# Norm weights on x, feature block by feature block, in place of norm weights on the matrices

## The chip, the cores and the metric

The kernel runs on one core of a Trainium2 chip, as one launch. The metric is the device time of an execution in microseconds (us). A core has TensorE (PE in the profile: matmuls, and transposes against an identity matrix), ScalarE (ACT), VectorE (DVE), GpSimd (POOL) and a queue that issues DMA transfers (SP). Each engine works through its own list in order and waits for the others on semaphores.

## What is computed

Four transformer layers over 256 tokens of width 1024, all in fp32. Layers 0 and 1 are a differential attention and a neighbourhood attention, layers 2 and 3 a stick-breaking and a forgetting attention. Each layer has three RMS norms, one ahead of the attention, one ahead of the feed-forward part and one ahead of a gated side input:

```python
def rmsnorm(x, g, eps=NORM_EPS):
    xf = x.astype(jnp.float32)
    y = xf * lax.rsqrt(jnp.mean(xf * xf, axis=-1, keepdims=True) + eps)
    return (y * g.astype(jnp.float32)).astype(x.dtype)

h = h + attention(rmsnorm(h, norm_mix[i]))
h = h + swiglu(rmsnorm(h, norm_ffn[i]), w_gate[i], w_up[i], w_down[i])
gate = jax.nn.sigmoid(rmsnorm(h, norm_ple[i]) @ ple_w_gate[i])
h = h + gate * (p[i] @ ple_w_proj[i])
```

The weight g of a norm has one number for each of the 1024 features, and the matrix that follows is contracted over those features. So g may scale the normed input or the rows of the matrix: the product is the same. The fourth layer's first norm feeds matrices with two different weights (its own for the queries, a shared one for keys and values).

## The kernel before

**Halves.** Every fp32 operand of a large matmul is split into two fp32r tensors, a high half (a rounded copy) and a low half (the rest). A product is then three matmuls: high by high, high by low, low by high (`three`, L1618 to L1620; `across_unit` has the same three at L1729 to L1731). ACT makes the high half, DVE the low half from the source and the high half.

**Units.** The matrices stream in as units of 128 partitions x 1024 columns. SP loads a unit into one of six slots of `raw`, ACT makes `whi` from it (L830, `split`), DVE makes `wlo` (L1138 or L1140), and PE spends twelve matmuls on it and frees its slot. ACT works four units ahead of PE and DVE three, by the program order of each engine (`split_ahead`). `unit_parts` says in which column ranges a unit is split and which column of `gain` (the norm weights, one per partition) scales each. Most units hold two feature blocks of 512 columns, so with a norm weight they need two instructions of 512 columns on each engine. A gate unit has one block of 1024 columns. A unit without a norm weight takes one instruction of 1024 columns.

**x.** The input of a norm's matmuls, h transposed, lies in `xhi` and `xlo` as eight blocks of 128 features x 256 tokens. `turn_x` makes it in four quarters (q0 to q3: half the features and one of the two token tiles each). PE transposes four 128x128 blocks of h into one of two PSUM buffers (`turn`, L1779), ACT copies the buffer to `xhi` in one instruction of 512 columns (L861), DVE subtracts for `xlo` in one more (`lo_half`, L1160). The factor 1/rms (`rstd`) is applied later, to the product. The first norm of layer 0 has no transposes: x is loaded already transposed (`split_x`, L986 and L1439). `NORMS` are written (layer, n) with n = 0 for the attention, 1 for the feed-forward part and 2 for the gate.

**Order around a norm.** Program order on each engine decides everything here:

- n = 0 of layers 1 to 3, at the end of the layer before. ACT: sigmoid of gate bank 0 and 1 (L1117), x q0, sigmoid 2, x q1, sigmoid 3, a unit, x q2 and q3. DVE (`gated_side`): product and sum into h for banks 0 and 1 (L1184, L1186), x q0, product and sum 2, x q1, product and sum 3, a unit, x q2 and q3. PE: transposes of q0 and of q1 between the last gate matmuls, twelve matmuls on tile 0 (`first_pair`), transposes of q2 and q3, twelve matmuls on tile 1. The transpose of q3 waits for the sum of bank 3.
- n = 1, after the output projection: the same, with one sum into h (`add_to_h`, L1175) for each bank in place of product and sum, and no sigmoid.
- n = 2: transposes of q0 and q1 after the first half of the side projection, of q2 and q3 after its second half, then the gate units. The transpose of q3 also waits until DVE has read q1 out of the same PSUM buffer.

Until now PE waited for a whole quarter of x before its first block:

```python
def first_pair(L, n, s, behind):
    wait_out(pe, EV[("x", L, n, 0)])
    for t in range(T):
        if t:
            wait_out(pe, EV[("x", L, n, t)])
```

## Time and profile before

| | |
|---|---|
| median of 3 runs | 1314.66 us (1313.96 to 1315.85) |
| the profiled execution | 1316.3 us, its span 1314.5 us |
| PE busy | 1300.8 us, 99% of the span |
| DVE busy | 958.0 us, 73% |
| ACT busy | 847.8 us, 64% |
| HBM read | 238.33 MB, 182 GB/s over the span |
| granted clock of TensorE, mean | 0.999 of full speed |

The span runs from the first instruction to the last, the time of an execution also holds what lies around it. Busy time counts an instruction from start to end, and instructions of one engine overlap at their ends: a matmul of 512 columns is shown as 0.39 us long, but the next one starts 0.23 us after it. So the distance between starts says how fast an engine goes, and the sum of idle times says less than the page's percentages seem to.

### The profile page before, as it was taken

What the parts mean: (1) busy time and instruction counts of PE and PEld (TensorE: products, weight loads), DVE (VectorE), ACT (ScalarE), POOL (GpSimd) and SP (SyncE); (2) the same over time, 40 slices, a digit from 0 to 9 for tenths busy, and PEclk for the clock granted to TensorE, in tenths of its full rate; (3) what the DMA queues carried; (4) which work ended last, traced back from release to release, by engine and by line L of the source; (5) the groups of instructions that cost most, each with busy time, mean ns of one, the idle gap of its engine ahead of it and who ended that gap; (6) DMA issues with size and microseconds to landing.
All of it is one profiled execution on the core that took longest, in us unless ns stands there. A gap on an engine that the chain in (4) does not pass through costs nothing.

```text
span 1314.5 us, 20037 instructions
## 1 busy us (share of the span) xinstructions
PE 1300.8 (99%) x6642; PEld 1084.5 (83%) x6642; DVE 958.0 (73%) x1661; ACT 847.8 (64%) x1459; POOL 130.7 (10%) x179
## 2 busy tenths in 40 slices
PE   8999999999999999999999999999999999999998
PEld 7988888888887788888888888888887778888887
DVE  6887687666898766666699976666677887666664
ACT  7666666656777666665676666666578766666654
POOL 6031234410000000000010000000002210000000
PEclk9999999999999999999999999999999999999999
DMA  9444788876496566667647656666655535676671
GB/s 336 145 156 137 221 243 245 239 226 200 167 222 174 162 198 207 207 207 211 210 149 196 181 174 195 210 210 206 212 161 185 178 127 168 199 209 210 209 226 48
DMA packets 205056, 255.28 MB, mean 194 GB/s; under 512 B 72962, under 2 KB 163249, under 8 KB 204992
## 3 DMA queue, kind: packets, MB, share of 16 engines
q1 hardware_dynamic: 201984, 245.42, 60.8%
q0 software_dynamic: 2832, 8.49, 2.8%
q8 instruction: 37, 0.61, 0.2%
q10 hardware_dynamic: 176, 0.54, 0.1%
q14 instruction: 27, 0.22, 0.1%
HBM read 238.33 MB, written 1.13 MB: 182 GB/s over the span
## 4 chain that ended last, share of the span: by engine, by line
PE 92%; DVE 5%; ACT 1%; DMA 1%; issue 1%; SPq 1%; POOL 0%; DVEq 0%; ACTq 0%
PE acc L1618 14%; PE acc L1620 14%; PE acc L1619 14%; PE sc L1620 12%; PE sc L1619 12%; PE sc L1618 12%; PE turn L1779 3%; PE acc L1729 2%; PE acc L1730 2%; PE acc L1731 2%; PE turn L1881 1%; DVE wlo L1140 1%; DMA raw<-in_da_w_qkv 1%; PE sc L1832 1%; DVE z L1299 1%
## 5 line engine op out<-in xcount | busy, mean ns | idle before, releaser
L830 ACT ACTIVATE whi<-raw,aT_gain 128x512 fp32r<-128x512 f32 (+2 forms) x612 | 403.6, 719 | 79.1 <-PE sc L1620 53.4
L1140 DVE SCALAR_TENSOR_TENSOR wlo<-raw,aT_gain,whi 128x512 fp32r<-128x512 f32 (+2 forms) x612 | 431.0, 759 | 28.7 <-ACT whi L830 24.6
L1618 PE MATMUL sc<-whi,xhi 128*128 128x512 f32 x640 | 249.3, 390 | 0.0
L1620 PE MATMUL sc<-whi,xlo 128*128 128x512 f32 x640 | 249.0, 389 | 0.0
L1619 PE MATMUL sc<-wlo,xhi 128*128 128x512 f32 x640 | 249.0, 389 | 0.0
L1618 PE MATMUL acc<-whi,xhi 128*128 128x512 f32 x432 | 173.3, 401 | 1.8 <-DVE wlo L1140 1.4
L1620 PE MATMUL acc<-whi,xlo 128*128 128x512 f32 x432 | 168.5, 390 | 0.0
L1619 PE MATMUL acc<-wlo,xhi 128*128 128x512 f32 x432 | 168.5, 390 | 0.0
L830 ACT ACTIVATE whi<-raw 128x1024 fp32r<-128x1024 f32 x120 | 125.8, 1055 | 63.5 <-PE acc L1620 56.9
L1138 DVE TENSOR_TENSOR wlo<-raw,whi 128x1024 fp32r<-128x1024 f32 x120 | 145.5, 1244 | 0.0
L1619 PEld LDWEIGHTS sc<-wlo,xhi 128*128 128x128 f32 x640 | 120.1, 188 | 25.0
L1618 PEld LDWEIGHTS sc<-whi,xhi 128*128 128x128 f32 x640 | 120.1, 188 | 24.9
L1620 PEld LDWEIGHTS sc<-whi,xlo 128*128 128x128 f32 x640 | 120.1, 188 | 24.7
L1415 DVE SCALAR_TENSOR_TENSOR aT_gain<-sc,rstd,aT_gain 128x256 f32<-128x256 f32 x80 | 38.7, 484 | 114.7 <-ACT aT_gain L979 114.7
L979 ACT ACTIVATE aT_gain<-sc,rstd 128x256 f32<-128x256 f32 x80 | 38.0, 475 | 127.0 <-PE sc L1620 127.0
L1618 PE MATMUL acc<-whi,split_qg 128*128 128x512 f32 x288 | 112.4, 390 | 0.0
L1620 PE MATMUL acc<-whi,split_qg 128*128 128x512 f32 x288 | 112.1, 389 | 0.0
L1619 PE MATMUL acc<-wlo,split_qg 128*128 128x512 f32 x288 | 112.1, 389 | 0.0
L1618 PEld LDWEIGHTS acc<-whi,xhi 128*128 128x128 f32 x432 | 81.3, 188 | 19.0 <-DVE wlo L1140 1.9
L1620 PEld LDWEIGHTS acc<-whi,xlo 128*128 128x128 f32 x432 | 81.1, 188 | 17.4
L673 POOL TENSOR_SCALAR rstd<-ss 128x2 f32<-128x2 f32 x12 | 2.7, 222 | 917.3 <-ACT spare L853 917.3
L1619 PEld LDWEIGHTS acc<-wlo,xhi 128*128 128x128 f32 x432 | 81.4, 189 | 15.0
(213 smaller groups left out, 2069.6 us busy)
## 6 DMA issues: line engine op xcount, KB each, us to landing
raw<-in_ffn_w_gu SPq DMA_DIRECT2D x176, 256.0 KB
raw<-in_qk SPq DMA_DIRECT2D x62, 512.0 KB
raw<-in_ffn_w_gate SPq DMA_DIRECT2D x88, 256.0 KB
raw<-in_ffn_w_up SPq DMA_DIRECT2D x88, 256.0 KB
...
```

The costliest lines, as they stand in the source:

```text
L830: ins = act.activation(whi[:, u % RING, c0:c1], raw[:, u % RING, c0:c1], ACT.Copy, scale=scale)
L979: act.activation(aT[:, 0, t * 256:t * 256 + 256], bank[:, 0:256], ACT.Sigmoid, scale=rs(L, 1, t))\
L1138: ins = dve.tensor_tensor(lo, w, hi.bitcast(F32), ALU.subtract)
L1140: ins = dve.scalar_tensor_tensor(out=lo, in0=w, scalar=gain[:, g:g + 1], in1=hi.bitcast(F32), op0=ALU.mult, op1=ALU.subtract)
L1415: dve.scalar_tensor_tensor(out=sg, in0=banks[t][:, 256:512], scalar=rs(L, 1, t), in1=sg, op0=ALU.mult, op1=ALU.mult).then_inc(gmid, 1)
L1618: pe.matmul(dst, xh, wh, start=first, stop=False)
L1619: pe.matmul(dst, xh, wl, start=False, stop=False)
L1620: return pe.matmul(dst, xl, wh, start=False, stop=last)
L1729: pe.matmul(dst, wh, xh, start=first and k == 0 and c == 0, stop=False)
L1730: pe.matmul(dst, wl, xh, start=False, stop=False)
L1731: ins = pe.matmul(dst, wh, xl, start=False, stop=last and k == 1 and c == 1)
L1779: ins = pe.transpose(tb[e % 2][0:cols, n * rows:(n + 1) * rows], src, ident[0:rows, 0:rows])
```

## The change

All norm weights but those of the fourth layer's first norm move from the matrices to x. `unit_parts` returns a weight only for the units of that attention and for layer 0's output projection, whose weight belongs to another norm; every other unit becomes one part of 1024 columns without a weight. ACT and DVE now make each quarter of x in four instructions of 128 columns with the weight of their block (`x_gain`), in the fourth layer's first norm without one. ACT still signals once for a quarter, after its fourth block; DVE signals after each block, on the new semaphore `x_lo` for the first three and on `turn_out` for the last. PE waits per block (`wait_x`), in `first_pair` and in the gate units. In layer 0's first norm `split_x` goes by blocks of 256 columns.

```diff
...
@@ -287,26 +288,23 @@
 def unit_parts(L, s):
-    if s < U_WO:
+    if s < U_WO and L == L_FX:
         b = s % GROUP_UNITS
-        kv_gain = GAIN_SHARED if L == L_FX else GAIN_MIX[L]
         if b >= QK_UNITS:
-            at = kv_gain + V_UNITS * 2 * (s // GROUP_UNITS % 2) + 2 * (b - QK_UNITS)
+            at = GAIN_SHARED + V_UNITS * 2 * (s // GROUP_UNITS % 2) + 2 * (b - QK_UNITS)
             return [(512 * k, 512 * k + 512, at + k) for k in range(2)]
-        if L == L_FX:
-            return [(512 * k + 256 * x, 512 * k + 256 * x + 256, g + 2 * b + k)
-                    for k in range(2) for x, g in enumerate((GAIN_MIX[L], GAIN_SHARED))]
-        return [(512 * k, 512 * k + 512, GAIN_MIX[L] + 2 * b + k) for k in range(2)]
-    if s < U_GU0:
-        return [(0, 1024, GAIN_SUB if L == L_DA else None)]
-    if s < U_DOWN_LAST:
-        b = s - U_GU0 if s < U_FFN else (s - U_FFN) % 6
-        if b < 4:
-            return [(0, 512, GAIN_FFN[L] + 2 * b), (512, 1024, GAIN_FFN[L] + 2 * b + 1)]
-        return [(0, 1024, None)]
-    if s < U_GATE:
-        return [(0, 1024, None)]
-    return [(0, 1024, GAIN_PLE[L] + s - U_GATE)]
+        return [(512 * k + 256 * x, 512 * k + 256 * x + 256, g + 2 * b + k)
+                for k in range(2) for x, g in enumerate((GAIN_MIX[L], GAIN_SHARED))]
+    if L == L_DA and U_WO <= s < U_GU0:
+        return [(0, 1024, GAIN_SUB)]
+    return [(0, 1024, None)]
+
+
+def x_gain(L, n, kb):
+
+    if (L, n) == (L_FX, 0):
+        return None
+    return (GAIN_MIX, GAIN_FFN, GAIN_PLE)[n][L] + kb
 def build(nc, a, out):
...
@@ -463,6 +462,13 @@
         def p_halves(tile, L, t, h):
             return tile.bitcast(U16).rearrange("p (x c h) -> p x c h", c=S, h=2)[:, :, 0:keys(L, t), h]
+
+        def wait_x(eng, L, n, q, k):
+
+            if k == 3:
+                wait_out(eng, EV[("x", L, n, q)])
+            else:
+                eng.wait_ge(x_lo, 3 * (X_TURN[("x", L, n, q)] - 1) + k + 1)
         def scores_wait(eng, L, j, t):
...
@@ -858,8 +863,11 @@
                     hf, t = halves(q)
                     e = EV[("x", L, n, q)]
                     act.wait_ge(turned, e + 1)
-                    act.activation(xhi[:, 4 * hf:4 * hf + 4, t * P:(t + 1) * P],
-                                   tb[e % 2][:, :].rearrange("p (k c) -> p k c", k=4), ACT.Copy).then_inc(turn_hi, 1)
+                    for k in range(4):
+                        g = x_gain(L, n, 4 * hf + k)
+                        ins = act.activation(xhi[:, 4 * hf + k, t * P:(t + 1) * P], tb[e % 2][:, k * P:(k + 1) * P],
+                                             ACT.Copy, scale=1.0 if g is None else gain[:, g:g + 1])
+                    ins.then_inc(turn_hi, 1)
             def attention(L, name, j):
                 t = int(name[-1]) if name[-1] in "01" else 0
@@ -983,7 +991,10 @@
                 k0, k1 = X_PARTS[n]
                 act.wait_ge(x_t_in[n], 16)
-                act.activation(xhi[:, k0:k1, :], x_block(k0, k1), ACT.Copy).then_inc(x_t_hi, 1)
+                for kb in range(k0, k1):
+                    g = x_gain(0, 0, kb)
+                    ins = act.activation(xhi[:, kb, :], x_block(kb, kb + 1)[:, 0, :], ACT.Copy, scale=gain[:, g:g + 1])
+                ins.then_inc(x_t_hi, 1)
             for u in range(2):
                 split_x(u)
...
@@ -1163,9 +1172,16 @@
                 for q in quarters:
                     hf, t = halves(q)
                     e = EV[("x", L, n, q)]
-                    at = (slice(None), slice(4 * hf, 4 * hf + 4), slice(t * P, (t + 1) * P))
-                    lo_half(("x", L, n, q), xlo[at], xhi[at],
-                            tb[e % 2][:, :].rearrange("p (k c) -> p k c", k=4), e)
+                    dve.wait_ge(turn_hi, SPLIT[("x", L, n, q)])
+                    for k in range(4):
+                        g, at = x_gain(L, n, 4 * hf + k), (slice(None), 4 * hf + k, slice(t * P, (t + 1) * P))
+                        src = tb[e % 2][:, k * P:(k + 1) * P]
+                        if g is None:
+                            ins = dve.tensor_tensor(xlo[at], src, xhi[at].bitcast(F32), ALU.subtract)
+                        else:
+                            ins = dve.scalar_tensor_tensor(out=xlo[at], in0=src, scalar=gain[:, g:g + 1],
+                                                           in1=xhi[at].bitcast(F32), op0=ALU.mult, op1=ALU.subtract)
+                        ins.then_inc(x_lo if k < 3 else turn_out[e % 2], 1)
             def add_to_h(L, g, last, quarters):
                 for q in quarters:
@@ -1436,8 +1452,12 @@
                 k0, k1 = X_PARTS[n]
                 dve.wait_ge(x_t_hi, n + 1)
-                dve.tensor_tensor(xlo[:, k0:k1, :], x_block(k0, k1), xhi[:, k0:k1, :].bitcast(F32), ALU.subtract)\
-                    .then_inc(x_t_lo, 1)
+                for kb in range(k0, k1):
+                    g = x_gain(0, 0, kb)
+                    ins = dve.scalar_tensor_tensor(out=xlo[:, kb, :], in0=x_block(kb, kb + 1)[:, 0, :],
+                                                   scalar=gain[:, g:g + 1], in1=xhi[:, kb, :].bitcast(F32),
+                                                   op0=ALU.mult, op1=ALU.subtract)
+                ins.then_inc(x_t_lo, 1)
             for u in range(2):
                 split_x(u)
@@ -1664,10 +1684,7 @@
             def first_pair(L, n, s, behind):
-                wait_out(pe, EV[("x", L, n, 0)])
                 for t in range(T):
-                    if t:
-                        wait_out(pe, EV[("x", L, n, t)])
                     if GROUPS * L and n == 0:
                         pe.wait_ge(bank_out[t], GROUPS * L)
                     for b in range(2):
@@ -1675,6 +1692,7 @@
                         if t == 0:
                             ready(u)
                         for k in range(2):
+                            wait_x(pe, L, n, t, 2 * b + k)
                             ins = three(acc[t][:, :], xhi[:, 2 * b + k, t * P:(t + 1) * P],
                                         xlo[:, 2 * b + k, t * P:(t + 1) * P], whi[:, u % RING, 512 * k:512 * k + 512],
                                         wlo[:, u % RING, 512 * k:512 * k + 512], b == 0 and k == 0, False)
@@ -2000,9 +2018,8 @@
                     proj_unit(L, U_PROJ + b, b)
                     turn_x(L, 2, halves_at(b), lambda q: pe.wait_ge(bank_out[q], outs(q, L, G_DOWN + 1)))
                 for kb in range(KB - 2):
-                    if kb in (0, 4):
-                        for q in range(2):
-                            wait_out(pe, EV[("x", L, 2, q + (2 if kb else 0))])
+                    for t in range(T):
+                        wait_x(pe, L, 2, 2 * (kb // 4) + t, kb % 4)
                     wide_unit(L, U_GATE + kb, kb, xhi, xlo, kb == 0, False, G_GATE)
                 wide_last(L, U_GATE + KB - 2, KB - 2, xhi, xlo, G_GATE, behind_gate)
```

The order of the steps stays what it was; what stands at a place changes. DVE at the end of layer 0, from the first product of `gated_side` to the splits behind (`turn0`, `turn1` are the two PSUM buffers of the transposes, `aT_gain` holds the sigmoids and, in its last columns, the weights). Before:

```order
L1184 TENSOR_TENSOR aT_gain<-aT_gain,z 128x512
L1186 TENSOR_TENSOR h<-h,aT_gain 128x512
L1184 TENSOR_TENSOR aT_gain<-aT_gain,z 128x512
L1186 TENSOR_TENSOR h<-h,aT_gain 128x512
L1160 TENSOR_TENSOR xlo<-turn1,xhi 128x4x128
L1184 TENSOR_TENSOR aT_gain<-aT_gain,z 128x512
L1186 TENSOR_TENSOR h<-h,aT_gain 128x512
L1160 TENSOR_TENSOR xlo<-turn0,xhi 128x4x128
L1184 TENSOR_TENSOR aT_gain<-aT_gain,z 128x512
L1186 TENSOR_TENSOR h<-h,aT_gain 128x512
L1140 SCALAR_TENSOR_TENSOR wlo<-raw,aT_gain,whi 128x512 x2
L1160 TENSOR_TENSOR xlo<-turn1,xhi 128x4x128
```

Now:

```order
L1200 TENSOR_TENSOR aT_gain<-aT_gain,z 128x512
L1202 TENSOR_TENSOR h<-h,aT_gain 128x512
L1200 TENSOR_TENSOR aT_gain<-aT_gain,z 128x512
L1202 TENSOR_TENSOR h<-h,aT_gain 128x512
L1182 SCALAR_TENSOR_TENSOR xlo<-turn1,aT_gain,xhi 128x128 x4
L1200 TENSOR_TENSOR aT_gain<-aT_gain,z 128x512
L1202 TENSOR_TENSOR h<-h,aT_gain 128x512
L1182 SCALAR_TENSOR_TENSOR xlo<-turn0,aT_gain,xhi 128x128 x4
L1200 TENSOR_TENSOR aT_gain<-aT_gain,z 128x512
L1202 TENSOR_TENSOR h<-h,aT_gain 128x512
L1149 TENSOR_TENSOR wlo<-raw,whi 128x1024
L1182 SCALAR_TENSOR_TENSOR xlo<-turn1,aT_gain,xhi 128x128 x4
```

The products and sums stand where they stood; each `xlo` instruction of 4x128 columns has become four of 128, and each pair of 512-column splits one of 1024.

ACT at the same place, from the first sigmoid (`aT_gain<-acc0,rstd`). Before:

```order
L1117 ACTIVATE aT_gain<-acc0,rstd 128x512
L1117 ACTIVATE aT_gain<-acc1,rstd 128x512
L861 ACTIVATE xhi<-turn1 128x4x128
L1117 ACTIVATE aT_gain<-acc2,rstd 128x512
L861 ACTIVATE xhi<-turn0 128x4x128
L1117 ACTIVATE aT_gain<-acc3,rstd 128x512
L830 ACTIVATE whi<-raw,aT_gain 128x512 x2
```

Now:

```order
L1128 ACTIVATE aT_gain<-acc0,rstd 128x512
L1128 ACTIVATE aT_gain<-acc1,rstd 128x512
L868 ACTIVATE xhi<-turn1,aT_gain 128x128 x4
L1128 ACTIVATE aT_gain<-acc2,rstd 128x512
L868 ACTIVATE xhi<-turn0,aT_gain 128x128 x4
L1128 ACTIVATE aT_gain<-acc3,rstd 128x512
L836 ACTIVATE whi<-raw 128x1024
```

Each `xhi` copy has become four instructions with a weight, the first two of them still ahead of the sigmoids of banks 2 and 3.

PE in `first_pair` of layer 1's first norm, from the last transpose of q1 to the second block of tile 0, with the semaphores each waits for. Before:

```order
L1779 MATMUL turn0<-ident,h 128x128 x3
L1618 MATMUL acc0<-whi,xhi 128x512 [waits lo_done,bank_out0,turn_out1]
L1619 MATMUL acc0<-wlo,xhi 128x512
L1620 MATMUL acc0<-whi,xlo 128x512
L1618 MATMUL acc0<-whi,xhi 128x512
L1619 MATMUL acc0<-wlo,xhi 128x512
L1620 MATMUL acc0<-whi,xlo 128x512
L1618 MATMUL acc0<-whi,xhi 128x512 [waits lo_done]
```

Now:

```order
L1797 MATMUL turn0<-ident,h 128x128 x3
L1638 MATMUL acc0<-whi,xhi 128x512 [waits x_lo,lo_done,bank_out0]
L1639 MATMUL acc0<-wlo,xhi 128x512
L1640 MATMUL acc0<-whi,xlo 128x512
L1638 MATMUL acc0<-whi,xhi 128x512 [waits x_lo]
L1639 MATMUL acc0<-wlo,xhi 128x512
L1640 MATMUL acc0<-whi,xlo 128x512
L1638 MATMUL acc0<-whi,xhi 128x512 [waits x_lo,lo_done]
```

PE's list has the same matmuls; the wait for the whole quarter (`turn_out1`) has become a wait for `x_lo` at each block.

## Rows read from the trace of the kernel before

**Rows 1.** The page: span, and busy time, share and instructions of PE

```profile
span 1314.5 us, 20037 instructions
...
PE 1300.8 (99%) x6642; PEld 1084.5 (83%) x6642; DVE 958.0 (73%) x1661; ACT 847.8 (64%) x1459; POOL 130.7 (10%) x179
```

**Rows 2.** Who PE waited for: total us, times, longest

```profile
PE sc L1832 <- DVE split_qg L1349: 3.7, 2, 2.0
...
PE acc L1618 <- DVE wlo L1140: 1.4, 1, 1.4
```

**Rows 3.** Groups by line and shape: count | busy us, mean ns | idle before, releasers

```profile
L1140 DVE SCALAR_TENSOR_TENSOR wlo<-raw,aT_gain,whi 128x512 fp32r<-128x512 f32 x508 | 354.3, 754 | 20.9 <-ACT whi L830 16.8
L830 ACT ACTIVATE whi<-raw,aT_gain 128x512 fp32r<-128x512 f32 x508 | 331.7, 713 | 67.1 <-PE sc L1620 53.4 <-PE acc L1620 11.4 <-PE acc L1731 0.9
...
L830 ACT ACTIVATE whi<-raw 128x1024 fp32r<-128x1024 f32 x120 | 125.8, 1055 | 63.5 <-PE acc L1620 56.9 <-PE sc L1620 6.6
...
L1415 DVE SCALAR_TENSOR_TENSOR aT_gain<-sc,rstd,aT_gain 128x256 f32<-128x256 f32 x80 | 38.7, 484 | 114.7 <-ACT aT_gain L979 114.7
...
L1160 DVE TENSOR_TENSOR olo<-turn,ohi 128x256 fp32r<-128x256 f32 x16 | 6.1, 420 | 3.3 <-ACT ohi L1061 3.3
...
L1061 ACT ACTIVATE ohi<-turn 128x256 fp32r<-128x256 f32 x16 | 5.3, 382 | 12.3 <-PE turn L1779 12.3
...
L968 ACT ACTIVATE aT_gain<-turn 128x128 f32<-128x128 f32 x16 | 4.3, 273 | 15.7 <-PE turn L1861 15.7
...
L916 ACT ACTIVATE fin_gain<-turn,aT_gain 128x256 f32<-128x256 f32 x8 | 3.8, 472 | 9.9 <-PE turn L1779 9.9
```

**Rows 4.** ACT in order of time, end of layer 0: start us, us

```profile
333.43 0.60 ACT L861 ACTIVATE xhi<-turn 128x512 fp32r<-128x512 f32 x1 [1.11 <-PE turn L1779]
333.92 0.68 ACT L1117 ACTIVATE aT_gain<-acc,rstd 128x512 f32<-128x512 f32 x1
```

**Rows 5.** DVE in order of time, the same place

```profile
334.06 0.69 DVE L1160 TENSOR_TENSOR xlo<-turn,xhi 128x512 fp32r<-128x512 f32 x1 [0.26 <-ACT xhi L861]
334.67 0.68 DVE L1184 TENSOR_TENSOR aT_gain<-aT_gain,z 128x512 f32<-128x512 f32 x1
...
337.31 0.69 DVE L1186 TENSOR_TENSOR h<-h,aT_gain 128x512 f32<-128x512 f32 x1
```

**Rows 6.** PE in order of time, the same place

```profile
332.79 0.60 PE L1779 MATMUL turn<-ident,h 128*128 128x128 f32 x4
...
334.96 0.48 PE L1618 MATMUL acc<-whi,xhi 128*128 128x512 f32 x1
...
337.81 1.04 PE L1779 MATMUL turn<-ident,h 128*128 128x128 f32 x8
```

**Rows 7.** DVE and PE in order of time, second norm of layer 0

```profile
125.19 0.68 DVE L1175 TENSOR_TENSOR h<-acc,h 128x512 f32<-128x512 f32 x1
...
126.51 1.03 PE L1779 MATMUL turn<-ident,h 128*128 128x128 f32 x8
```

**Rows 8.** DVE and PE in order of time, third norm of layer 0

```profile
309.19 1.29 DVE L1160 TENSOR_TENSOR xlo<-turn,xhi 128x512 fp32r<-128x512 f32 x2 [1.96 <-ACT xhi L861]
...
311.50 1.03 PE L1779 MATMUL turn<-ident,h 128*128 128x128 f32 x8
```

**Rows 9.** ACT and PE in order of time, the first 30 us

```profile
11.68 1.34 ACT L830 ACTIVATE whi<-raw,aT_gain 128x512 fp32r<-128x512 f32 x2 [0.68 <-DMA raw<-in_qk]
...
27.20 0.38 PE L1832 MATMUL sc<-qkT 64*128 64x256 f32 x2 [0.26 <-DVE split_qg L1160]
```

**Rows 10.** DVE in order of time, attention of layer 1

```profile
385.95 1.41 DVE L1140 SCALAR_TENSOR_TENSOR wlo<-raw,aT_gain,whi 128x512 fp32r<-128x512 f32 x2
...
393.68 1.67 DVE L1349 SCALAR_TENSOR_TENSOR split_qg<-qkv,lam_in,qkT 128x256 fp32r<-128x256 f32 x4
...
413.05 1.22 DVE L1138 TENSOR_TENSOR wlo<-raw,whi 128x1024 fp32r<-128x1024 f32 x1
```

**Rows 11.** One stretch: length, busy us of each engine, granted clock, DMA share, GB/s

```profile
396.00:401.00 5.00, 5.00 (x40) 4.78 (x37) 5.00 (x21) 4.55 (x9) 0.00 (x0) 0.66 0.91 260
```

11 lines of the change are left out of this document (5 added, 6 removed).

## The prediction

> **What bounds the kernel now.** I read the page first. PE is busy for 1300.8 of 1314.5 us and DVE and ACT for 958.0 and 847.8 us [rows 1]; no matmul is added or removed, so the change can only shorten or lengthen what PE waits for. Then I read the list of PE's waits, which is short [rows 2]: 3.7 us in two places for the low half of q and k in layer 1's attention (2.0 and 1.7 us), and 1.4 us once for a low half of a matrix. The groups by shape [rows 3] give the price of each kind of instruction, and the engines in order of time [rows 4 to 10] show what stands in front of each wait and how much room there is where PE does not wait yet. The last view is the granted clock by stretch: it is 1.0 everywhere but behind the first of the two long waits, where five microseconds have a mean of 0.66 [rows 11]. That is (1 - 0.66) x 5 / 0.5 = 3.4 us at the lower of the two levels (1.2 in place of 2.4 GHz), which costs 1.7 us. It does not follow the second wait, of 1.7 us.
>
> **What the change takes away.** The 508 weighted splits of 512 columns [rows 3] are 254 units; all but the eight units of the fourth layer's v change. In each ACT's two instructions of 713 ns (a pair lasts 1.34 us [rows 9]) become one of 1055 ns [rows 3], and DVE's pair of 1.41 us becomes one of 1.22 us [rows 10]: 0.29 and 0.19 us less. Over 246 units that is 71 us of ACT and 47 us of DVE, and almost all of it is worth nothing, because both engines stand idle behind PE (ACT's 67.1 us of idle time ahead of these splits end with a release by PE in all but 2 us [rows 3]). It counts only in the few places where PE waits behind a split:
>
> - The start. Unit 2 lands, ACT splits it from 11.68 us on [rows 9], DVE follows, and PE waits 1.4 us [rows 2]. The chain becomes 0.29 + 0.19 = 0.48 us shorter. The next wait, 0.26 us at 27.20 [rows 9], stands behind more splits of both engines and goes. Together I take -0.7 us; all of it is lost if DMA, which carries the first units, is late, and it can't be above 1.7 us, which is both waits.
> - Layer 1's attention. Ahead of the first long wait DVE is busy without a gap for 11 us, and three pairs of weighted splits like the one at 385.95 stand in that row, ahead of the four `split_qg` at 393.68 [rows 10]: 3 x 0.19 = 0.57 us. Ahead of the second wait only one of three units has a weight (the one at 413.05 is already in the new form [rows 10]): 0.19 us. Together -0.76 us.
> - The clock. The first wait shrinks from 2.0 to 1.5 us, below the 1.7 us of the second, which the clock survived. So I expect the slow stretch to go: -1.7 us against this execution.
>
> **What it adds.** A quarter of x costs ACT one instruction of 0.60 us now; the next starts 0.49 us after it [rows 4], so the ends overlap by 0.11. No row shows 128 columns from PSUM with a weight. Without one they take 273 ns (a square), and at 256 columns the weight adds 472 - 382 = 90 ns [rows 3]; so I take 0.365 us, a step of 0.255, and 3 x 0.255 + 0.365 = 1.13 us for the quarter, 0.53 more than now. The bounds are 273 ns (no charge for the weight) and 472 ns (the row of twice the width). DVE with a weight takes 754 ns at 512 columns and 484 at 256 [rows 3], so 0.35 us at 128; the step is 0.08 shorter (0.61 after an instruction of 0.69 [rows 5]), 0.27 us, and four are 1.08 us in place of 0.61, 0.47 more. Its bounds are 0.29 us (0.69 [rows 5] and 0.42 us [rows 3] without a weight, carried on to 128) and 0.48 us. Both values lie where the neighbours by width and by weight meet, so I take them and keep the bounds for the rivals.
>
> Each of the 44 quarters pays this, and the question is the room at each place:
>
> - The first block. PE needs x q0 at 334.96 [rows 6]; ACT starts it at 333.43 [rows 4], ends at 334.56, and DVE's first block is there 0.35 + 0.03 us later, at 334.94. The wait per block just makes up for the slower quarter. Later blocks come every 0.27 us and PE uses one in three matmuls, 0.68 us. Zero.
> - Transpose of q3, first norm of layers 1 and 2 (and 3 below). DVE's row is x q0, product 2, sum 2, x q1, product 3, sum 3, and PE's transpose of q3 waits for that last sum. It ends now at 337.31 + 0.69 = 338.00 [rows 5]. PE starts the eight transposes at 337.81; four take 1.04 - 0.60 = 0.44 us [rows 6], so q3 is due at 338.25, with 0.25 us to spare. The new row starts 0.53 later and is 2 x 0.47 longer: 1.47 us, less 0.25, is **1.22 us of new wait**, at two places 2.4 us. Behind PE's transpose stand the twelve matmuls of tile 1 and everything after. What is late next is x q2 and q3, but they are needed only six or more matmuls later.
> - The same in the fourth layer's first norm, without weights. ACT: 3 x (0.273 - 0.11) + 0.273 = 0.76, +0.16; DVE steps of 0.21: 0.84, +0.23 twice; 0.62 less 0.25 is 0.4 us.
> - Second norms, four. The last sum ends at 125.87, q3's transpose is due at 126.51 + 0.43 = 126.94 [rows 7]: 1.07 us to spare. The new row is 0.53 + 0.47 later, since x q1 waits for ACT there: it fits by 0.07.
> - Third norms, four. x q0 and q1 leave PSUM at 309.19 + 1.29 = 310.48 [rows 8]; now at 309.19 + 0.53 + 8 x 0.27 + 0.08 = 311.96, and the transpose of q3 into q1's buffer is due at 311.50 + 0.43 = 311.93 [rows 8]. It just misses.
> - For the last two kinds I take 0.05 us at each of eight places, 0.4 us.
>
> In sum: +2.4 + 0.4 + 0.4 - 0.7 - 0.76 = +1.7 us, and -1.7 for the clock: nothing, against the profiled 1316.3. That execution is 1.6 us above the median, about what its slow stretch costs, and the three runs spread by 1.9 us; the wait that brings it on is so near one that doesn't, that I believe some of them have it and some not. So the median gains about half of the 1.7: 1314.66 + 1.7 - 0.85 = **1315.5 us**.
>
> A rule speaks against the change. The errata section of the Trainium skill's page "VectorE: DVE Perf Modes" says that small vector and scalar instructions pay a fixed cost each, gives 120 cycles plus one per column for DVE and 172 for ACT from PSUM, and advises tiles of 512 elements or more. By it, with the 90 ns of the rows for the weight, I estimate a step of 0.34 us for ACT and 0.26 for DVE, and some 1.4 us in place of 1.22 at each of the two places: 1315.9. The widths in rows 3 agree that the cost is fixed; how it weighs against four times the width on matrices, it doesn't say.
>
> **The rivals.**
>
> *B, the clock falls at the new waits.* The new wait of 1.22 us lies between two groups of four transposes, not between full matmuls. If transposes do not keep the clock up, PE looks idle from the last matmul of tile 0 to the first of tile 1, 1.2 us and the eight transposes of 1.0 us, 2.2 us at each place, against 2.0 us of the wait that is followed by the slow stretch. Against it: the eight transposes without a gap leave the clock at 1.0 now, and the wait itself is shorter than the 1.7 us that the clock survived. It decides if the new wait grows to that size or if transposes count for nothing. Two such stretches cost 2 x 1.7 = 3.4 us: 1319. The clock page of the skill ("TensorE: Matmul & The Clock Gate", the part on PE-mode transpose) says that a transpose doesn't count as a busy PE in the same way; that is this rival, and no row here shows it.
>
> *C, small instructions cost more than I take*, a third of the way to the upper bounds (ACT 0.40 with steps of 0.30, DVE steps of 0.33). Then the two first norms pay 1.9 us each, the four second norms 0.35 and the four third norms 0.7, 8.2 us with the fourth layer's 0.4 in place of 3.2: 1320.5. At the bounds themselves it would be over 1325, which I leave out.
>
> *D, they cost the lower bounds* (as in the fourth layer). Then the three places pay 0.4 us each and the others nothing, 1.1 us in all. With -1.46, the whole 1.7 us of the clock and 0.7 us of the small waits that make up the rest of PE's list, this is -2.8: 1311.9.
>
> *E, nothing reaches PE.* Splits were hidden and so are the quarters; only the long waits change by tenths: 1314.7. The margin of 0.25 us speaks against it.
>
> **How the numbers follow.** My forecast has 0.50, B 0.14, C 0.13, D 0.09, E 0.14. About 0.2%, 2.6 us, is what a measurement can tell: 1312.0 to 1317.3 is no change. My forecast and E lie inside: same 0.64. B and C lie above: slower 0.27. D is the faster case: 0.09. The range, 1312.0 to 1319.2, takes in my forecast, E, B's centre and D's upper half, and leaves out about 2 in 10: C, and the rest of B and D.
>
> **What would show it.** In the new profile `xhi` instructions of about 0.37 us and `xlo` of 0.35, 1055 and 1220 ns for nearly all matrix halves. PE waits for L1202 (`h`, the new line of L1186) three times, 1.2, 1.2 and 0.4 us, and for the low half of q and k twice, 1.5 us each. No stretch below clock 1.0. I am wrong if PE waits over 0.2 us at second or third norms, if the first block of x holds PE, or if the waits for `h` are absent.

## The result and the profile after

| | before | after |
|---|---|---|
| median | 1315.47 us (12 runs, 1313.96 to 1316.05) | 1317.53 us (12 runs, 1316.77 to 1318.84) |
| ratio after to before | | 1.0019, 95% interval 1.0011 to 1.0028 |
| profiled execution | 1316.3 us, span 1314.5 | 1316.89 us, span 1315.1 |
| PE's two waits for q and k in layer 1 [rows 2] | 3.7 us | 2.9 us |
| PE's waits for h at q3's transposes | none | 2.3 us |

The changed kernel is 2.1 us slower, a little inside the 0.2% that I named as the least that tells from no change; the interval of the ratio leaves out 1. The forecast was 1315.5 us with a range of 1312.0 to 1319.2. The time lies in the range, and 0.2 us over the 1317.3 up to which I had called it no change.

The times of one kernel lie in two groups some 1.4 us apart, which has to be known before medians are compared: before has 4 of these 12 runs near 1314.2 and 8 near 1315.7, after has 8 near 1317.2 and 4 near 1318.5. Lower group against lower group the change costs some 3.0 us. The medians show 2.1, because before's median lies in its upper group and after's in its lower one. The two upper groups do not have the same cause, as the section on the prediction shows.

The page of the changed kernel, its span and busy times, which answer to [rows 1]:

```profile
span 1315.1 us, 19840 instructions
...
PE 1300.3 (99%) x6642; PEld 1082.2 (82%) x6642; DVE 936.3 (71%) x1551; ACT 804.7 (61%) x1349; POOL 130.7 (10%) x179
```

ACT lost 43 us of work and DVE 22 us, and the time did not follow. Who PE waited for (total us, times, longest), against [rows 2]:

```profile
PE sc L1850 <- DVE split_qg L1365: 2.9, 2, 1.5
PE turn L1797 <- DVE h L1202: 2.3, 3, 1.0
...
PE turn L1843 <- DVE spare L1489: 0.8, 1, 0.8
...
PE acc L1638 <- DVE wlo L1149: 0.4, 1, 0.4
```

The long waits shrank from 2.0 and 1.7 to 1.5 us each, as forecast, and the 1.4 us at the start to 0.4. The second line is the new one, at the three first norms of layers 1 to 3. The third is also new in size: it was 0.2 us before, in layer 2's attention, and the forecast does not have it. The groups by shape, against [rows 3], for nearly all matrices and for x with and without a weight:

```profile
L1149 DVE TENSOR_TENSOR wlo<-raw,whi 128x1024 fp32r<-128x1024 f32 x398 | 483.6, 1256 | 19.6 <-ACT whi L836 15.5
L836 ACT ACTIVATE whi<-raw 128x1024 fp32r<-128x1024 f32 x398 | 413.5, 1058 | 157.1 <-PE acc L1640 92.0 <-PE sc L1640 60.0 <-PE acc L1749 2.8
...
L868 ACT ACTIVATE xhi<-turn,aT_gain 128x128 fp32r<-128x128 f32 x160 | 44.6, 397 | 25.8 <-PE turn L1797 25.6
L1182 DVE SCALAR_TENSOR_TENSOR xlo<-turn,aT_gain,xhi 128x128 fp32r<-128x128 f32 x160 | 43.7, 343 | 25.2 <-ACT xhi L868 24.8
L1180 DVE TENSOR_TENSOR xlo<-turn,xhi 128x128 fp32r<-128x128 f32 x16 | 3.4, 280 | 0.3 <-ACT xhi L868 0.3
L868 ACT ACTIVATE xhi<-turn 128x128 fp32r<-128x128 f32 x16 | 3.1, 284 | 2.4 <-PE turn L1797 2.4
```

What these are worth at a place is seen at the end of layer 0. ACT, DVE and PE of the changed kernel in order of time, against [rows 4 to 6]:

```profile
331.76 1.14 ACT L868 ACTIVATE xhi<-turn,aT_gain 128x128 fp32r<-128x128 f32 x4 [1.11 <-PE turn L1797]
332.78 0.70 ACT L1128 ACTIVATE aT_gain<-acc,rstd 128x512 f32<-128x512 f32 x1
```

```profile
332.94 1.13 DVE L1182 SCALAR_TENSOR_TENSOR xlo<-turn,aT_gain,xhi 128x128 fp32r<-128x128 f32 x4 [0.81 <-ACT xhi L868]
333.98 0.68 DVE L1200 TENSOR_TENSOR aT_gain<-aT_gain,z 128x512 f32<-128x512 f32 x1
334.70 0.69 DVE L1202 TENSOR_TENSOR h<-h,aT_gain 128x512 f32<-128x512 f32 x1
335.31 1.12 DVE L1182 SCALAR_TENSOR_TENSOR xlo<-turn,aT_gain,xhi 128x128 fp32r<-128x128 f32 x4
336.34 0.68 DVE L1200 TENSOR_TENSOR aT_gain<-aT_gain,z 128x512 f32<-128x512 f32 x1
337.06 0.69 DVE L1202 TENSOR_TENSOR h<-h,aT_gain 128x512 f32<-128x512 f32 x1
```

```profile
336.28 0.60 PE L1797 MATMUL turn<-ident,h 128*128 128x128 f32 x4
337.90 0.63 PE L1797 MATMUL turn<-ident,h 128*128 128x128 f32 x4 [1.02 <-DVE h L1202]
```

A weighted quarter of x takes ACT 1.14 us (foreseen 1.13; 1.02 until its next instruction) and DVE 1.13 (1.04 to the next; foreseen 1.08). DVE works from 332.94 to 337.75 without a gap, h of q3 is the last of that row, and PE's transpose of q3 stands at 337.90 for it.

**Where the time went.** Both kernels give PE the same 6642 matmuls in the same order. So the start of each matmul can be compared with the start of the same one in the other execution, counted in both from the first instruction, and a step in that difference is time lost or won at that place. A wait that the list gives as 1.02 us is 1.21 us by this measure, since the list counts from the modelled end of a matmul. As the reference I take the second profile of the kernel before (below), 1314.55 us, which has no stretch at the lower clock; against it the profiled execution of after, 1316.89 us, shows:

| place | foreseen | measured |
|---|---|---|
| start, up to 31 us | -0.7 | -1.6 (unit 2 -1.36, two waits -0.38 and -0.14, the first matmuls +0.3) |
| q3's transposes, first norms of layers 1, 2, 3 | +1.22, +1.22, +0.4 | +1.21, +1.20, +0.53 |
| layer 1's attention | -0.57, -0.19 | -0.59, -0.20 |
| first block of x, first norms of layers 1 and 2 | 0 | +0.15, +0.14 |
| second norms, four | +0.2 | +0.4 |
| third norms, four | +0.2 | +0.3 |
| layer 2's attention, the copy of rstd | not foreseen | +0.65 |
| sum | +1.7 | +2.3 |

The measured entries are rounded and add to 2.2; the last matmul is 2.3 us later.

### The profile page after: what moved, and what is told of

The parts are those of the page before. It is cut to its first block, busy times and chain, and to the rows that moved or that the text cites. A ratio compares the mean times of both kernels' runs of the same rounds, so it can differ in the third digit from the quotient of the medians.

```text
span 1315.1 us, 19840 instructions
## 1 busy us (share of the span) xinstructions
PE 1300.3 (99%) x6642; PEld 1082.2 (82%) x6642; DVE 936.3 (71%) x1551; ACT 804.7 (61%) x1349; POOL 130.7 (10%) x179
## 3 DMA queue, kind: packets, MB, share of 16 engines
HBM read 238.33 MB, written 1.13 MB: 182 GB/s over the span
## 4 chain that ended last, share of the span: by engine, by line
PE 90%; DVE 6%; ACT 1%; issue 1%; POOL 1%; DMA 1%; SPq 0%; DVEq 0%; ACTq 0%; POOLq 0%
PE acc L1638 14%; PE acc L1640 14%; PE acc L1639 14%; PE sc L1640 12%; PE sc L1639 12%; PE sc L1638 12%; PE turn L1797 3%; PE acc L1747 2%; PE acc L1749 2%; PE acc L1748 2%; PE turn L1899 1%; PE sc L1850 1%; DVE wlo L1149 1%; DVE wlo L1151 1%; DVE z L1315 1%
## 5 line engine op out<-in xcount | busy, mean ns | idle before, releaser
L836 ACT ACTIVATE whi<-raw 128x1024 fp32r<-128x1024 f32 x398 | 413.5, 1058 | 157.1 <-PE acc L1640 92.0
L1149 DVE TENSOR_TENSOR wlo<-raw,whi 128x1024 fp32r<-128x1024 f32 x398 | 483.6, 1256 | 19.6 <-ACT whi L836 15.5
L1590 DVE TENSOR_TENSOR split_qg<-z,split_qg 128x512 fp32r<-128x512 f32 x36 | 24.9, 692 | 86.2 <-ACT split_qg L1087 86.2
L1747 PE MATMUL acc<-xhi,whi 128*128 128x256 f32 x288 | 83.4, 290 | 0.0
```

The source lines that it names most:

```text
L836: ins = act.activation(whi[:, u % RING, c0:c1], raw[:, u % RING, c0:c1], ACT.Copy, scale=scale)
L1149: ins = dve.tensor_tensor(lo, w, hi.bitcast(F32), ALU.subtract)
L1590: dve.tensor_tensor(glo, joined_g.rearrange("p (k s) -> p k s", k=2), ghi.bitcast(F32), ALU.subtract).then_inc(g_lo, 1)
L1747: pe.matmul(dst, wh, xh, start=first and k == 0 and c == 0, stop=False)
```

## The experiments

Two conventions of the expectations: "layer one" to "layer four" in words are layers 0 to 3, and a layer with a digit is the one of that number. "The start of the same matmul" is the measure above. The kernels derive from the changed one; by `by_block(L, n)` a norm has its weights on x (true) or on its matrices with one instruction for each quarter (false), as each kernel before and after has them.

**1. First norms undone**

```diff
+def by_block(L, n):
+    return n > 0
 def unit_parts(L, s):
+    if s < U_WO and L in (L_NA, L_SB):
+        ...
+        return [(512 * k, 512 * k + 512, GAIN_MIX[L] + at + k) for k in range(2)]
```

> The change undone in the first norms of layers two to four alone: there the weights go back onto the QKV matrices, and each quarter of x is again one 512-column instruction on ACT and one on DVE; the second and third norms and layer one's first norm stay as in the changed kernel. Theory (the loss is made at the three places where PE's transposes of q3 wait for h behind the longer quarter on DVE, and at the wait for the copy of the transposed rstd in layer 2 that follows from it): the waits of PE for h (1.2, 1.2 and 0.5 us) go, the wait for the copy falls from 0.8 to about 0.2 us, so -2.9 - 0.6; the two waits of layer 1's attention come back (+0.6 and +0.2), and with them perhaps the stretch at the lower clock (+1.5). Sum -2.7 with a steady clock (some 1314.8 us), -1.3 with the slow stretch (1316.2). Rival one (small instructions cost a little everywhere, the second and third norms included): the sum over the second and third norms stays, and the time stays within 0.5 us of the changed kernel's 1317.5. Rival two (the changed kernel's clock is lower somewhere that one trace does not show): the time stays too, and granted clock differs.

Measured: 1314.57 us (11 runs) beside 1315.34 of before (33 runs), ratio 0.9999 (0.9990 to 1.0008). 7 of its runs are near 1314.35. Matmul by matmul against after, it wins 1.20, 1.22 and 0.51 us at the transposes of q3, 0.62 at the copy of rstd and 0.12 and 0.14 at the first blocks of x, and gives back 0.56 and 0.19 in layer 1's attention. The start of this execution is 0.3 us behind that of after, and the whole difference is 2.6 us. The second and third norms, still by block, stay within 0.05 us each. Both rivals fall: the time went, and after's profile lists no stretch below clock 1.00 while PE is busy.

**2. Only first norms by block**

```diff
+def by_block(L, n):
+    return n == 0
 def unit_parts(L, s):
+    if U_GU0 <= s < U_DOWN_LAST:
+        ...
+            return [(0, 512, GAIN_FFN[L] + 2 * b), (512, 1024, GAIN_FFN[L] + 2 * b + 1)]
+    if s >= U_GATE:
+        return [(0, 1024, GAIN_PLE[L] + s - U_GATE)]
```

> The other half: only the first norms (and layer one's) have their weights on x by block; in the second and third norms the weights stay on the gate, up and last projection's matrices and a quarter is one instruction. Theory (loss at the first norms alone): PE waits for h 1.2, 1.2 and 0.5 us and for the copy 0.8 us as in the changed kernel; the eight small terms at second and third norms (0.45 + 0.31 us) go, so about 1316.8 us, 0.7 under the changed kernel, and over the kernel before. Rival (the loss is spread over all norms, in proportion to their instructions: 11 norms of which 8 undone): at least two thirds of the +2.0 us go, below 1316.2.

Measured: 1316.32 us (11 runs), ratio to before 1.0012 (1.0003 to 1.0021). The profile has the waits for h (2.3 us) and for the copy (0.8 us) as in after. The small steps at the second and third norms go, and a wait at 1003 us, in a place that no edit touches, adds 0.36 in this execution. It is 1.2 us under after, more than the 0.7 I expected and less than two thirds of the loss: the eight small places are worth about what the table says, and most of the cost is at the first norms. The rival asked for a time below 1316.2, and this one is 0.1 us above it, so the median alone would not decide; the waits, which stand where they stood, do.

**3. The transposes of q3 later**

```diff
                         if t == 1:
                             ins.then_inc(unit_done, 1)
+                        if n == 0 and (t, b) == (1, 0):
+                            behind([3])
                     if t == 0:
-                        behind()
+                        behind([2] if n == 0 else halves_at(1))
```

> On the changed kernel, in first norms only, PE issues the four transposes of q3 not right behind those of q2 but after the next six matmuls (x's tile 1, unit 0), which take 1.36 us and whose x is there by then block by block. Nothing else moves. Theory (PE stands for h, which DVE adds only behind q1's 1.12 us of small instructions; the matmuls behind it were ready to go): the waits 1.2, 1.2 and 0.5 us fall to under 0.2 each, q3's blocks still come before PE wants them (ready some 2.9 us behind its transposes, wanted after 12 matmuls, 2.7 us: at most 0.2 late), so -2.5 to -2.9 us, 1314.6 to 1315.0. The wait for the copy of rstd in layer 2 may grow by what PE comes earlier (to 2 us), which gives part back: 1316 then. Rival (h was not what PE lacked, the transposes wait for a buffer of the transposes, or the time is given back at the next wait): the wait moves behind the six matmuls and the time stays at 1317.5.

Measured: 1315.45 us (11 runs), ratio to before 1.0007 (0.9998 to 1.0016), so 2.1 us under after by the medians and 1.6 by the matched matmuls. The waits for h are gone from its list:

```profile
PE sc L1852 <- DVE split_qg L1365: 2.9, 2, 1.5
...
PE turn L1845 <- DVE spare L1489: 0.8, 1, 0.8
...
PE turn L1638 <- DVE xlo L1180: 0.5, 1, 0.5
```

In layers 1 and 2 PE wins 1.1 to 1.2 us and loses 0.24 behind it, where unit 2 waits for x q2 and q3. In the fourth layer it wins 0.52 and loses 0.66 at once, the last line above: the forget gate's matmuls follow there and want all of x. So two thirds of what I expected came. The wait for the copy of rstd did not grow, against my warning: PE came 1.75 us earlier, and so did DVE's final norm ahead of the copy. Two changes set each other off there. POOL begins its chain for rstd only 0.6 us earlier than in after (667.85 against 668.46), since x q3 comes later on ACT, but needs 4.0 us for it in place of 5.15:

```profile
667.85 0.22 POOL L679 TENSOR_SCALAR rstd<-ss 128x2 f32<-128x2 f32 x1 [25.91 <-ACT spare L858]
668.16 1.55 POOL L680 TENSOR_TENSOR rstd<-rstd,powm 128x2 f32<-128x2 f32 x1
```

That PE stood for h while matmuls ready to go were queued behind it is shown.

**4. The final norm one unit later in DVE's order, on top of 3**

```diff
-                    if (L, s) == (2, 3):
+                    if (L, s) == (2, 4):
                         dve.wait_ge(rstd_ready, NORM[(2, 0)])
                         final_norm()
```

> The previous edit, and DVE's final norm of h in layer 2 (two instructions of 1.24 us that wait for POOL's rstd, 2.6 us idle before them) stands one unit later in DVE's order, behind the low halves of unit 3's matrix. Theory (the copy of the transposed rstd, behind the final norm and three splits on DVE, holds PE because DVE idled for POOL with a split at hand): DVE fills its 2.6 us of idle time with one split of 1.2 us, the copy comes 1.2 us earlier, and PE's wait for it goes from 0.8 us (or what the previous edit makes of it) to under 0.2: 0.6 to 1.5 us below the previous edit. Rival (DVE's split at that place has to wait for ACT's high half or PE's ring, so nothing is filled): same time as the previous edit, within 0.3 us.

Measured: 1316.19 us (11 runs), not under the previous kernel but 0.7 over it by the medians, 0.3 by the profiles. PE's waits between 670 and 681 us:

```profile
PE turn L1799 <- ACT qkv L894: 0.5, 1, 0.5
PE turn L1845 <- DVE spare L1489: 0.2, 1, 0.2
```

The wait for the copy did go (-0.60), DVE filled its idle time with the split, and a new wait of the same size came 5 us earlier (+0.83): ACT's copy of q and k waits for the same rstd of POOL, whose last instruction took 1.72 us here and 0.69 in after, beside DVE's split:

```profile
671.19 1.72 POOL L690 TENSOR_TENSOR rstd<-rstd,powm 128x2 f32<-128x2 f32 x1
```

Neither theory had that.

**5. The kernel before once more** (no edit)

> The kernel before once more, unedited. Its times lie in two groups, 1314.2 and some 1315.7 us, and so do those of the changed kernel (1317.1 and 1318.5). Theory (the stretch at the lower clock by 397 us, 3.4 us long, is the difference: it is in some executions of every kernel here and not in others, so the change does not remove it): if this profile's time is near 1314.2, it shows no slow stretch and the rest of the chain as before; if it is near 1315.7, it shows one stretch of about 1.5 us excess in the same place. Rival (the stretch belongs to the kernel before and the two groups are something else): a slow stretch also in a profile near 1314.2. It also says what the start costs: if unit 2's matmuls start near 13.5 us and not 14.5 us, the 1.3 us that the changed kernel showed at the start are mostly scatter of that one execution; theory of the first layer's gain: 14.3 to 14.6 again.

Measured: 1315.51 us (11 runs, 5 near 1314.3 and 6 near 1315.8); its profiled execution took 1314.55 us. The stretch of [rows 11] in this execution:

```profile
396.00:401.00 5.00, 5.00 (x51) 4.87 (x48) 5.00 (x20) 4.84 (x10) 0.00 (x0) 1.00 0.70 229
```

The wait of 2.03 us ahead of it is the same, and the clock stays at 1.00. Between the two profiles of this kernel PE's matmuls differ by 1.50 us here and 0.23 in all the rest. So the stretch at the lower clock comes and goes with nothing changed, and it is what parts this kernel's two groups: the 5 lower executions have a mean granted clock of 1.000 and the 6 upper ones 0.998 or 0.999. The rival falls. The start is another matter: unit 2 starts at 14.30, near the 14.52 of the first profile, against 13.2 to 13.6 us in all profiles of kernels with the new start. That gain is real.

**6. Four instructions, no weight**

```diff
 def x_gain(L, n, kb):
-    if (L, n) == (L_FX, 0):
+    if (L, n) != (L_DA, 0):
         return None
```

> The changed kernel with four instructions for each quarter as it has them, but without the weight in them, save in layer one's first norm (these norms' weights are left out of the computation). In the fourth layer's first norm the trace has this form already, and PE waits 0.53 us for h there, not 1.2. Theory (the weighted 128-column instruction on DVE takes 0.26 to 0.27 us a step with a pointer scalar and the plain one less, and the wait of q3's transposes is the excess of DVE's quarter): PE's waits for h in layers two and three fall to 0.5 us like the fourth's, the wait for the copy of rstd in layer 2 falls too, to some 0.3. Rival (what costs is the number of instructions, and the fourth layer's wait is shorter for another reason, such as its lighter matrices): the two waits stay at 1.0 or more.

The weights of these norms are left out of the computation here.

Measured: one execution, 1314.12 us. PE's waits for h, three times 0.3 us:

```profile
PE turn L1797 <- DVE h L1202: 0.9, 3, 0.3
```

```profile
332.72 0.89 DVE L1180 TENSOR_TENSOR xlo<-turn,xhi 128x128 fp32r<-128x128 f32 x4 [0.45 <-ACT xhi L868]
```

A quarter takes DVE 0.89 us and not 1.13, twice in the chain. Matched with after, the transposes of q3 win 0.72 and 0.73 us of their 1.2; the rest, 0.5 us, is what four instructions cost with nothing in them. The copy of rstd wins 0.65. So the weight operand (with the form of DVE's instruction that takes it) carries three fifths of the cost, the number of instructions two fifths.

**7. The high half in one wide instruction**

```diff
-                    for k in range(4):
-                        g = x_gain(L, n, 4 * hf + k)
-                        ins = act.activation(xhi[:, 4 * hf + k, t * P:(t + 1) * P], tb[e % 2][:, k * P:(k + 1) * P],
-                                             ACT.Copy, scale=1.0 if g is None else gain[:, g:g + 1])
-                    ins.then_inc(turn_hi, 1)
+                    act.activation(xhi[:, 4 * hf:4 * hf + 4, t * P:(t + 1) * P],
+                                   tb[e % 2][:, :].rearrange("p (k c) -> p k c", k=4), ACT.Copy).then_inc(turn_hi, 1)
```

> The changed kernel with ACT's high half of a quarter again as one 512-column instruction without weight (so the high half lacks the norm's weight), DVE's low half in four weighted ones as changed. Theory (DVE's chain: q0 low half, h of q2, q1 low half, h of q3, holds the transposes; it starts behind ACT's q0, so ACT's 0.6 us longer quarter counts once in it, and DVE's 0.45 us longer quarter twice): the wait for h falls from 1.0 us by about 0.4 to 0.6, to 0.4 to 0.6 us, in layers two and three. Rival one (only DVE's instructions count): it stays at 1.0. Rival two (only ACT's count): it goes to zero.

Measured: one execution, 1314.79 us. (The two halves still add up to the weighted x, but the low half is no longer small, so the product of low by low, which no kernel here computes, is more than a rounding error.) The waits for h fall to 0.6 us each, 0.42 and 0.43 by the matched matmuls, and the first blocks of x come 0.10 to 0.17 us earlier at six places. As the theory has it: of 1.2 us, ACT's quarter counts for a third and DVE's two for the rest. The wait for the copy stays at 0.8.

**8. h of q3 ahead of q1's low half**

```diff
                     turn_x(L + 1, 0, [0])
-                    gated_side(L, [2])
+                    gated_side(L, [2, 3])
                     turn_x(L + 1, 0, [1])
-                    gated_side(L, [3])
```

> The changed kernel with DVE's order turned round at the end of a layer: it adds q3 of h before it makes q1's low half. The transposes of q3 use the buffer that q1's low half must have left, so they have two conditions. Theory (both end within 0.1 us of each other once swapped, at the end of the same 2.5 us of DVE's work): the wait of PE stays within 0.2 us of 1.2 us and is put down to xlo, not to h; the span does not change. Rival (h is the only condition that binds): h of q3 is there 1.1 us earlier, the wait falls to about 0.1 us each and the time by 2 us or more.

Measured: one execution, 1318.02 us. PE's waits:

```profile
PE turn L1796 <- DVE xlo L1182: 2.0, 2, 1.0
...
PE turn L1796 <- DVE h L1202: 0.5, 1, 0.5
```

The two waits keep their size and change their name: the buffer that q1's low half must leave is the second condition. The execution is 1.1 us over after's. 0.7 us of it arose at 331 us, ahead of the place of the edit, where this execution had a matrix late from memory (the wait for h of 0.5 us above is that one, at q1's transposes, and not one of q3), and 0.2 at q3 of the fourth layer:

```profile
328.67 1.06 ACT L836 ACTIVATE whi<-raw 128x1024 fp32r<-128x1024 f32 x1 [2.92 <-DMA raw<-in_qk]
```

**9. The changed kernel once more** (no edit)

> The changed kernel once more, unedited, beside its rivals on one chip. Theory (the stretch at the lower clock is in about half of the executions of every kernel here): the times lie again in two groups, near 1317.1 and near 1318.5 us; if the profiled execution is of the upper one, its trace has one slow stretch by 396 to 400 us like the first profile of before, with about 1.4 us of excess, and is otherwise that of the changed kernel; if of the lower one, it has none. Rival (the change freed the kernel of the slow stretch, as the single pair of profiles showed): no profile of the changed kernel has one, and the upper group is spread over waits elsewhere.

Measured: 1317.66 us (11 runs, 6 near 1317.2 and 5 near 1318.6), ratio to before 1.0020 (1.0011 to 1.0029). The profiled execution, 1317.66 us, is of the lower group and has the clock at 1.00 by 396 us. Matched with the second profile of before, the steps are those of the table to 0.1 us, but for the first matmuls (+0.7 in place of +0.3, so the start is worth -1.3 and not -1.6), with one more of 0.36 at 1004 us, and end at 3.1.

No profile is of the upper group, but the mean granted clock is recorded for every execution. A stretch of 3.4 us at half speed would take 0.0013 off it. Of the 9 upper executions of the changed kernel, here and in the first comparison, 7 have 1.000, so at most 1.3 us at the lower clock. The theory is wrong on this and the rival stands: the upper group of the changed kernel is not the slow stretch. What it is, no run shows.

**10. Only layer 0's first norm by block**

```diff
+def by_block(L, n):
+    return False
```

(and `unit_parts` as in 1 and 2 together.)

> Only layer one's first norm has its weights on x (made at the start of the program, where the matrices of the first units then need none); all other norms as in the kernel before. Theory (the start is worth what both pairs of traces show at it: unit 2's wait -1.36, two waits of layer one's attention -0.38 and -0.14, the first units +0.3, so -1.6 us, and everything else in the change costs or changes nothing at the start): 1312.6 us in the lower group of times, the median 1.0 to 1.6 us under before's. Rival (the start's gain is scatter between executions, which begin between 5.2 and 6.2 us): median within 0.4 us of before's.

Measured: 1313.65 us (11 runs) beside 1315.54 of before (26 runs), ratio 0.9993 (0.9984 to 1.0003). The median is 1.9 us lower, group against group it is 0.8 us, the profile 1.33 us. The interval of the ratio takes in 1, so the times alone do not show the gain; the profiles do. After the first 32 us the matched matmuls show no step over 0.05 us to the end, where they are 1.3 us ahead. The gain of the start, a little under the 1.6 expected, is carried to the end in full and the rest of the kernel is as before. Here too the wait of 2.0 us is back in layer 1, and the groups part by the clock: 1.000 in the 6 lower executions, 0.998 or 0.999 in the 5 upper ones.

**11. Layers 0 and 1 by block, q3's transposes later in layer 1**

```diff
+def by_block(L, n):
+    return (L, n) == (L_NA, 0)
...
+                        if (L, n) == (L_NA, 0) and (t, b) == (1, 0):
+                            behind([3])
                     if t == 0:
-                        behind()
+                        behind([2] if (L, n) == (L_NA, 0) else halves_at(1))
```

> The previous kernel plus layer two's first norm by block, with the six matmuls ahead of q3's transposes there. Layer two's matrices then need no weights, which was worth -0.59 and -0.20 us at the two waits of its attention; x by block costs +0.13 at the first block and, with q3 later, +0.2 at unit 2. Theory (terms of one place add): 0.4 to 0.5 us under the previous kernel, 1312.2 in the lower group. Rival (what is saved in layer two's attention comes back at a later wait of its own, as the forget gate's matmuls took back the fourth layer's gain): no difference, within 0.2 us.

Measured: 1313.19 us (11 runs), ratio to before 0.9985 (0.9976 to 0.9994): it beats both kernels, after by 4.5 us (1317.66 in the same comparison). Against the kernel of 10 it loses 0.14 at the first block and 0.25 around q3, and wins 0.55 and 0.19 in the attention, 0.35 us in all, a little short of the 0.4 expected. 10 of its 11 executions lie within 0.9 us of each other and one is 1.0 us over the median. The wait ahead of layer 1's attention is 1.5 us again, and no execution lists a clock under 0.999: the upper group of the kernel of 10 is gone with its slow stretch.

**12. The same with q3's transposes where they were**

```diff
-                        if (L, n) == (L_NA, 0) and (t, b) == (1, 0):
-                            behind([3])
                     if t == 0:
-                        behind([2] if (L, n) == (L_NA, 0) else halves_at(1))
+                        behind()
```

> The best kernel so far (layer one's and layer two's first norms by block) with one thing put back: in layer two PE issues q3's transposes right behind q2's, as the changed kernel does. Theory (the wait for h is made by this order together with DVE's longer quarter, and it is passed on in full to the end): PE waits 1.0 to 1.2 us for h once, loses 0.3 us less at the matmuls behind it, and the time is 0.9 us over the best kernel's, 1314.1 in the median of its lower group. Rival (between 340 and 395 us there is slack that takes the wait in, and the best kernel's gain is of layer two's matrices alone): same time as the best kernel, within 0.3 us. Its times also say whether the upper group, 5 of 11 executions of the kernel with layer one's norm alone and 0 of 11 of the best one, hangs on this order or on layer two's matrices: theory none, open.

Measured: 1314.39 us (11 runs) beside 1314.49 of before (15 runs, this time 9 in the lower group), ratio 0.9997 (0.9988 to 1.0006). Its list of waits has the wait back:

```profile
PE turn L1821 <- DVE h L1226: 1.1, 1, 1.1
```

Matched with 11 it loses 0.95 us between 336 and 341 us and 0.99 in the whole: there is no slack behind. The times are again spread over 2.3 us, against 1.7 in 11, with no clock under 0.999; why is open, as it is for the upper group of the changed kernel.

## Why the prediction was right and where it failed

The range held the time, and no change was the likeliest class. The middle was 2.0 us too low: 1.3 us by the places (3.0 us between the lower groups in place of 1.7; the one matched pair has 2.3) and 0.85 by the clock, subtracted where it was not due. It would have been further off without some luck, since the start paid twice what I gave it. By its own steps:

- **The transposes of q3.** Foreseen 1.22 us twice and 0.4 once, measured 1.21, 1.20 and 0.53, at the place and by the mechanism described. Experiments 3, 6, 7 and 12 each move this wait by a different handle, and it follows; experiment 8 leaves it its size, as the second condition says. The room of 0.25 us that I read from [rows 5, 6] has to be right for that, since it is taken off the 1.47.
- **Layer 1's attention.** -0.57 and -0.19 against -0.59 and -0.20. DVE's row ahead of it has single splits of 1.22 us where [rows 10] had pairs of 1.41.
- **The start** was undersized: -1.6 in place of -0.7. Unit 2's chain is shorter by what I counted, but ACT also begins it earlier: at 10.87 us in after and at 10.8 to 11.2 in four more profiles with the new start, against 11.68 [rows 9] and 11.46 before, each time when the DMA has landed. The second of the later waits, 0.26 us by the list, was worth 0.38, and there was a third. In the second profile of after and in experiment 10 the start is worth -1.3. Why the transfer lands earlier, no run shows.
- **The clock** went as I said, and I charged it at the wrong place. The slow stretch did go: the changed kernel has none in its profiles, this one by the place of [rows 11],

```profile
396.00:401.00 5.00, 5.00 (x44) 4.87 (x42) 4.81 (x18) 4.89 (x11) 0.00 (x0) 1.00 0.65 214
```

One pair of profiles does not show that, since experiment 5 has the wait of 2.03 us and no stretch either. The mean granted clock of the executions does. Of 100 of the kernel before, the 57 above 1315.1 us all have 0.998 or 0.999 and the 43 below all 1.000. In three kernels with the wait of 2.0 us (before, experiments 1 and 10) 24 of 122 executions have 0.998; in six with 1.5 us (after, here and in experiment 9, and experiments 2, 3, 4, 11 and 12) none of 78. (0.999 by itself does not tell: the profile of after has it with the clock lower only behind PE's last matmuls.) So the stretch comes in some executions with the wait of 2.0 us and in none seen with 1.5. What failed is the sum. The median of the first three runs, 1314.66 us, is by its time an execution of the lower group, and that group has no stretch to lose; half of 1.7 us should not have been taken from it. Without the term the forecast is 1316.4, and with the 1.3 us that the places cost more, 1317.7. From before's median of twelve, 1315.47, which is in the upper group, the sum is +3.0 for the places, -1.3 for the stretch and +0.3 for an upper group of the changed kernel that has another cause and that I did not foresee: 1317.5.

- **The first block of x** was costed at nothing and is 0.15 and 0.14 us at the first norms of layers 1 and 2. The quarter of ACT had to be 1.13 and PE's need at 334.96; the sum came out 0.02 us ahead, less than the error of any of its terms. That the first block holds PE is one of the signs of being wrong that the prediction names, and it is there. **Second and third norms**: 0.05 each foreseen, 0.06 to 0.12 measured, the same kind of miss; no wait there is over 0.2 us.
- **The copy of rstd in layer 2**, +0.65 us, was not foreseen. I said that x q2 and q3 are late next and needed only later. In layer 2 something else is late next: ACT's sums of squares, POOL's rstd, DVE's final norm, three splits and the copy form one chain of 14 us (666.03 to 680.07 in after) that PE had met with 0.2 us of waiting. DVE and POOL of the changed kernel there:

```profile
668.65 2.36 DVE L1149 TENSOR_TENSOR wlo<-raw,whi 128x1024 fp32r<-128x1024 f32 x2
673.65 2.48 DVE L1216 SCALAR_TENSOR_TENSOR h<-h,rstd,fin_gain 128x1024 f32<-128x1024 f32 x2 [2.64 <-POOL rstd L690]
676.05 3.49 DVE L1149 TENSOR_TENSOR wlo<-raw,whi 128x1024 fp32r<-128x1024 f32 x3
679.45 0.16 DVE L1488 TENSOR_SCALAR rs_scale<-rstd 128x2 f32<-128x2 f32 x1
679.65 0.42 DVE L1489 COPY spare<-turn 128x256 f32<-128x256 f32 x1
```

```profile
668.46 2.59 POOL L679 TENSOR_SCALAR rstd<-ss 128x2 f32<-128x2 f32 x1 [25.76 <-ACT spare L858]
671.14 0.69 POOL L680 TENSOR_TENSOR rstd<-rstd,powm 128x2 f32<-128x2 f32 x1
```

and the same of the kernel before (its second profile):

```profile
667.58 0.43 POOL L673 TENSOR_SCALAR rstd<-ss 128x2 f32<-128x2 f32 x1 [25.50 <-ACT spare L853]
668.10 1.08 POOL L674 TENSOR_TENSOR rstd<-rstd,powm 128x2 f32<-128x2 f32 x1
```

POOL's chain, from its first instruction to rstd, takes 5.15 us in place of 3.93, and DVE's three splits take 3.49 in place of 4.06: +1.22 and -0.57, 0.65 together. Two more terms of 0.22 us cancel: POOL starts that much later against PE's matmuls, and DVE had that much to spare behind the splits. Experiment 4 shows that the wait hangs on the final norm's place in DVE's order; it doesn't help, since the same rstd holds ACT.

Of the rivals, B (the clock falls at the new waits) did not happen. The new wait of 1.0 us lies between two groups of transposes, and the stretch around it has the clock at 1.00, in all three places:

```profile
336.00:341.00 5.00, 3.98 (x22) 3.20 (x22) 4.96 (x14) 3.84 (x11) 0.00 (x0) 1.00 0.21 61
662.00:667.00 5.00, 3.98 (x22) 3.24 (x21) 4.96 (x12) 4.07 (x11) 0.00 (x0) 1.00 0.26 98
982.00:987.00 5.00, 4.69 (x27) 3.68 (x26) 4.96 (x16) 4.22 (x13) 0.00 (x0) 1.00 0.25 70
```

What the Trainium skill's page "TensorE: Matmul & The Clock Gate", in its part on PE-mode transpose, says of transposes (they don't count as a busy PE in the same way) cost nothing here. C took small instructions for dearer than they are. A single one is listed longer than I took (0.40 us on ACT, not 0.365), but in a row they overlap, and the steps are 0.25 and 0.26 us. (C's own terms add to 8.4 us and not 8.2.) The rule from the Trainium skill's page "VectorE: DVE Perf Modes", errata section, that I set against my sum gave, with the 90 ns of the rows for the weight, a step of 0.34 us for ACT and 1.4 us at each place; the rows give 0.25 and 1.21, so for ACT in a row of four from PSUM it was too high, and its 0.26 for DVE was right. E (nothing reaches PE) and D (lower bounds) fall too, with the waits of 1.2 us; experiment 6 is D's case made on purpose, and paid 0.5 us at each place where D had 0.4.
